# Six lower halves of weights made by GpSimd instead of VectorE at the end of the first block's mixers

## The reference, cut to what matters

```
merged = (gates[:, :, 0] * einsum('bsk,kd->bsd', a, w_br_mla)
          + gates[:, :, 1] * einsum('bsk,kd->bsd', b, w_br_moba)
          + gates[:, :, 2] * einsum('bsk,kd->bsd', c, w_br_dil))
return einsum('bsd,de->bse', merged, w_out)
```

## Time and profile before

| | us |
|---|---|
| median of 3 runs | 2763.22 (2762.93 to 2763.27) |
| profiled execution, its own time | 2762.27 |
| its span in the trace | 2760.5 |
| TensorE busy | 2746.0 (99%) |
| VectorE busy | 1821.8 (66%) |
| ScalarE busy | 1465.4 (53%) |
| GpSimd busy | 211.3 (8%) |

### The profile page before, as it was taken

The page is one execution under the profiler, slowest core; times in us unless marked ns, Lnnn a source line. Parts: engine busy times, 40 slices in busy tenths (PEclk is TensorE's granted clock), DMA queues, the critical chain, the costliest instruction groups (busy, mean ns, idle before and its releaser), DMA issues.

```text
span 2760.5 us, 44842 instructions
## 1 busy us (share of the span) xinstructions
PE 2746.0 (99%) x18188; PEld 2456.5 (89%) x18188; DVE 1821.8 (66%) x2892; ACT 1465.4 (53%) x2404; POOL 211.3 (8%) x156
## 2 busy tenths in 40 slices
PE   9999999999999999999999999999999999999998
PEld 8989879989989789989998887899899888878997
DVE  6656765646556856656577877765565678787755
ACT  6545645545455645444456566454444566665442
POOL 0010001010010010010012100110100121001100
PEclk9999999999999999999999999999999999999999
DMA  6544445555544445555555444555555554445653
GB/s 248 198 171 162 152 159 197 188 185 194 199 170 159 152 162 212 199 188 202 193 190 189 140 181 145 213 199 199 196 200 189 192 183 153 161 167 179 218 198 122
DMA packets 75069, 504.10 MB, mean 183 GB/s; under 512 B 8784, under 2 KB 10480, under 8 KB 19184
## 3 DMA queue, kind: packets, MB, share of 16 engines
q1 hardware_dynamic: 74576, 501.06, 50.9%
q10 hardware_dynamic: 288, 0.17, 0.0%
HBM read 500.12 MB, written 1.08 MB: 182 GB/s over the span
## 4 chain that ended last, share of the span: by engine, by line
PE 93%; DVE 4%; ACT 1%; issue 1%; DMA 0%; SPq 0%; DVEq 0%; ACTq 0%
PE ps L1667 47%; PE ps L1687 40%; PE ps L1708 3%; DVE wlo L2166 1%; DVE conv L2439 1%; PE ps L1803 1%; PE ps L1828 1%; PE ps L1801 1%; ACT whi L1903 1%; ACT conv L2069 0%; PE ps L1830 0%; DMA raw<-in_w 0%; PE ps L1852 0%; DVE g L2377 0%; DVE oT_lo L2502 0%
## 5 line engine op out<-in xcount | busy, mean ns | idle before, releaser
L1903 ACT ACTIVATE whi<-raw 128x1024 fp32r<-128x1024 f32 (+3 forms) x938 | 976.4, 1043 | 616.8 <-PE ps L1667 402.6
L2166 DVE TENSOR_TENSOR wlo<-raw,whi 128x1024 fp32r<-128x1024 f32 (+2 forms) x894 | 1080.5, 1215 | 275.3 <-ACT whi L1903 274.3
L1687 PE MATMUL ps<-xT_both,whi 128*128 128x256 f32 x6848 | 857.0, 278 | 0.0
L1687 PEld LDWEIGHTS ps<-xT_both,whi 128*128 128x128 f32 x6848 | 813.3, 188 | 6.8 <-issue 5.3
L1667 PE MATMUL ps<-whi,xT_both 128*128 128x512 f32 (+2 forms) x2176 | 585.3, 390 | 0.5 <-ACT xT_both L1926 0.3
L1667 PEld LDWEIGHTS ps<-whi,xT_both 128*128 128x128 f32 x2176 | 397.2, 188 | 81.0 <-issue 9.0
L1687 PE MATMUL ps<-xT_both,wlo 128*128 128x256 f32 x3424 | 459.4, 277 | 0.0
L1687 PEld LDWEIGHTS ps<-xT_both,wlo 128*128 128x128 f32 x3424 | 421.3, 188 | 0.0
L1667 PE MATMUL ps<-wlo,xT_both 128*128 128x512 f32 (+2 forms) x1088 | 331.3, 386 | 0.3 <-DVE wlo L2166 0.3
L1667 PEld LDWEIGHTS ps<-wlo,xT_both 128*128 128x128 f32 x1088 | 202.1, 188 | 38.9 <-DVE wlo L2166 1.4
L1667 PE MATMUL ps<-whi,hT_hi 128*128 128x512 f32 x704 | 221.4, 390 | 0.0
(11 more groups left out here) (306 smaller groups left out, 2140.0 us busy)
## 6 DMA issues: line engine op xcount, KB each, us to landing
raw<-in_w SPq DMA_DIRECT2D x435, 1024.0 KB, 4.8
vr<-in_vrows SPq DMA_DIRECT2D x19, 512.0 KB, 5.6
raw<-in_w SPq DMA_DIRECT2D x12, 768.0 KB, 4.3
raw<-in_w SPq DMA_DIRECT2D x10, 896.0 KB, 4.5
sums<-scratch SPq DMA_DIRECT2D x8, 512.0 KB, 4.4
raw<-in_w SPq DMA_DIRECT2D x4, 832.0 KB, 4.6
raw<-in_w SPq DMA_DIRECT2D x4, 576.0 KB, 3.7
raw<-in_w SPq DMA_DIRECT2D x4, 512.0 KB, 6.7
```

Source lines behind the costliest of these rows:

```text
L1687: made = e.matmul(out, ws[:, o:o + 128], xs[:, kt, :], start=kt == 0 and n == 0 and c % 2 == 0, stop=kt == job.nk - 1 and n == 2, skip_gro ...
L1903: e.activation(out, raw, ACT.Copy).then_inc(*mark("hi", i))
L2166: e.tensor_tensor(out, raw, hi.bitcast(F32), sub).then_inc(*mark("lo", i))
```

## The change

When the first half (n = 0) of the last of the three branch products is about to be emitted in the mixer of the first block, three piece numbers are put into `on_pool`. The branch product has four pieces left at that point (`u` to `u + 3`), so the three numbers are pieces 0, 1 and 2 of `w_out`. It happens in both layers. (A `merge` of VectorE then stands at L2379 and L2384 instead of L2377 and L2382.)

```diff
         for i, (r, nk) in enumerate(order):
             for n in (0, 1):
                 banks, free = self.two()
+                if key == "br1" and i == len(order) - 1 and n == 0:
+                    self.on_pool |= set(range(self.u + NHL - 1, self.u + NHL + 2))
```

## The result

The changed kernel takes a median of **2769.53 us** (2767.15 to 2772.05, 12 runs) against 2762.94 (2762.12 to 2763.84, 12 runs) for the kernel before: a ratio of 1.0022 with a 95% interval of 1.0014 to 1.0029. That is 6.6 us more. The forecast was 2766.2 with a range up to 2768.5. The direction and the table of turns were right; the size was not, and one step of the prediction failed.

A forecast was written before the change was run, and what follows sets the result against it. The prediction took TensorE to bound the kernel, busy 2746.0 of 2760.5 us. Its terms, +1.93 + 0.10 - 0.53 = 1.50 us a layer, 3.0 in both, gave a median of 2766.2 us, range 2763.0 to 2768.5.

The forecast's parts named there:

- table of turns: Mixer ends: VectorE's adds and GpSimd's lower halves exclude each other and alternate; 1.50 us a layer, 2766.2 us, 82%.
- three terms: Per layer: transposes of t = 1 +1.93 us, late transposed-xn half for `w_out` +0.10, vanished wait at second column half -0.53.
- A: Mixer ends: no exclusion between VectorE's adds and GpSimd's lower halves; all waits vanish, 2.4 us won, 2760.8 us; 7%.
- B: Mixer ends: GpSimd keeps the turn, the first add waits for all three lower halves; 9.2 us in all, 2772.4; 5%.
- What was cost at nothing: Pieces 0 to 2 of `w_out`: GpSimd's lower halves come before TensorE wants them, later block-buffer reloads are covered; 0 us.
- rival C: TensorE's granted clock falls in the 2.2 us gap before the transposes of t = 1; 5 us more, 2771; 4%.

The follow-up runs named there:

- filled kernel: The changed kernel with 9 useless 128x512 matmuls in TensorE's gap before the waiting transposes, both layers; 2767.78 us against 2763.26 for the kernel before.
- fourth profile of the change: The changed kernel profiled a fourth time, without further edit; against the first profile of the kernel before, layer 1 lost 2.99 us and layer 2 lost 2.82.

## Where the prediction was right, and where it failed

**The table of turns held.** The prediction had GpSimd's second and third lower half at about 2.8 us (2.79 and 2.84), VectorE's adds at 2.0, 2.2, 2.2 and 0.69 (2.03, 2.12, 2.17, 0.69), one wait of about 2.2 us a layer (2.10) and none at the second column half. The three terms make 1.50 a layer; the traces of the change show 1.61 where the clock held. In the first layer the rows above give +1.95, +0.25 and -0.58 for the terms of +1.93, +0.10 and -0.53, so the second, the late lower half of the transposed xn, was the one set too small. With that the rivals A (adds of 0.69 us) and B (a first add of over 6 us) are excluded. What was cost at nothing held as well: the waits of TensorE for a lower half (L2168) are one of 0.3 us in the whole program, in the kernel before as in the change. The Trainium skill's wider rule (SBUF — State Buffer, Who interferes with whom), two SBUF inputs of VectorE against GpSimd's reads, fits these rows (2.03 instead of 0.69 us); the narrower note about two-port modes does not foresee them.

**The step that failed is rival C's dismissal:** "A gap of 2.2 us is shorter than that, and the clock should hold", at 4%. The gap came out at 2.10 us, and the clock fell behind it in five of eight cases, and in the one case of the second layer alone. The bound taken from the earlier trace rows was no bound: it is the delay of one fall after the last matmul of the program, and says only that the clock can stay up that long, not that it must. The Trainium skill's warning about gaps between bursts (TensorE: Matmul & The Clock Gate, HAM oscillation — how this bites in real kernels) stood beside it, and the runs agree that an idle gap brings the fall; but the gaps that the page warns of are longer than this one, so by its words, too, this gap would have passed. The 2.10 us measured here decide. The price of C was off too, the other way: 2.5 us a layer was forecast, 1.2 to 1.4 were measured, since the clock was low from 410.5 to 413.9, for instance, and not for 5 us. Both errors together: at five falls in eight, two layers lose 2 x 0.63 x 1.3 = 1.6 us on an average. With 3.2 for the collision that is 4.8 us, where 3.0 was forecast. By itself this would put the median at about 2767.7, still inside the range; that it came out above 2768.5 needs what stays open below, for which the prediction had no term.

**What stays open** is the difference between that and the medians of the change, which were 2768.40 to 2770.67 in four sets of runs, 5.2 to 7.4 us above the kernel before in the same set. Between 0.4 and 2.6 us are thus not accounted for, by a sum that rests on few profiles. The filled kernel, with no fall in its profile, is 4.5 us above before where its layers give 3.3. What the profiles offer for it lies behind the edit (the column "the rest", 0.5 to 1.2 us in most profiles of the change and of the filled kernels). One part of it comes with the edit: in the second block's first mixer a normalizing step of VectorE (L2232 after the change) starts 0.35 us later behind GpSimd's small instruction on the row sums (`stat`), and the transposes of x behind it delay TensorE by 0.3. First the kernel before, then the change, with the two instructions:

```profile
1404.60 0.56 POOL L2604 TENSOR_TENSOR stat<-stat,phalf 128x1 f32<-128x1 f32 x1
1405.23 0.75 DVE L2230 SCALAR_TENSOR_TENSOR x<-ps,stat,vr 128x512 f32<-128x512 f32 x1
```

```profile
1413.25 0.57 POOL L2606 TENSOR_TENSOR stat<-stat,phalf 128x1 f32<-128x1 f32 x1
1414.23 0.75 DVE L2232 SCALAR_TENSOR_TENSOR x<-ps,stat,vr 128x512 f32<-128x512 f32 x1 [0.47 <-POOL stat L2606]
```

The delay of 0.3 us is in all ten profiles of kernels with the edit in both layers and in none of the other four; why is not known. The other part is the slower pace of TensorE, in steps of up to 0.4 us and as whole feed-forward stages of about 4 us. The fourth profile of the change has one in the sixth of the eight such stages; first the kernel before, then the change:

```profile
1840.00:1870.00 30.00, 30.00 (x267) 30.00 (x266) 17.27 (x23) 14.86 (x22) 0.00 (x0) 1.00 0.52 182
```

```profile
1840.00:1870.00 30.00, 30.00 (x257) 30.00 (x257) 17.03 (x23) 14.81 (x22) 0.00 (x0) 1.00 0.56 199
```

The kernel before has runs some 3 to 5 us above its others as well (3 of 22, 4 of 27 and 3 of 21 in the last three sets, none of 45 in the first ones). Whether the change makes them more frequent wasn't shown, and so the cause of the remainder stays open.

## What to carry to other kernels

Before work is given to an idle engine, look in the trace for what the two engines' instructions do to each other at that place: here the lower halves cost 1.6 us a layer beside VectorE's two-input adds, and gained 0.9 in the traces when they were only started after the adds on which TensorE waits. Where a forecast contains a new gap of some 2 us in TensorE, price the gap with and without a fall of the clock and give both a real chance; one fall seen elsewhere in a trace is no threshold. And a single profile can mislead on a change of 0.2%: the first one here showed no fall of the clock, and 5.0 us that lay ahead of the edit.

## What was not expected of the hardware

- The same gap of 2.10 us is followed by a granted clock of 0.50 in some executions and of 1.00 in others of the same kernel. In the windows of the profiles with falls, the clock fell at times between 0.4 us before and 1.4 us after TensorE began again; it doesn't come at a fixed delay from the last matmul. In the second layer of the fourth profile of the change it was low already when the transposes began, and four of them took 1.11 us instead of 0.66:

```profile
1015.43 1.11 PE L1710 MATMUL ps<-ident,xn 128*128 128x128 f32 x4 [2.10 <-DVE xn L2384]
```

- At a granted clock of 1.00 and with no engine waiting, the matmuls with 256 columns of the feed-forward stages ran at one of two paces, 113.3 or 117.8 ns from start to start, for a whole stage: 267 or 257 to 258 in 30 us.
